# First block's norms taken apart: gains tile by tile, 1/rms later, on other engines

## The chip, the cores and the metric

The kernel runs on one core of a Trainium2 chip. It is a Bass program with one instruction queue per engine: TensorE (PE; its weight loads are PEld), VectorE (DVE), ScalarE (ACT), GpSimd (POOL) and SyncE (SP), which issues the loads. The engines meet only at semaphores. The metric is the device time of one execution in microseconds; three runs of the kernel before gave 1871.84 to 1873.96, median 1873.42.

## The reference, cut to what matters

Two blocks follow each other. The change is in the first: two layers over 272 tokens (16 meta tokens and 256), width 1024, and a closing norm.

```python
def rms_norm(x, g):
    y = xf * lax.rsqrt(jnp.mean(xf * xf, axis=-1, keepdims=True) + NORM_EPS)
    return (y * g.astype(jnp.float32)).astype(x.dtype)

def hybrid_layer(h, pos, norm_g, w_in, ...):
    u = rms_norm(h, norm_g)
    proj = jnp.einsum('bld,dp->blp', u, w_in)
    dq, dk, dv, dz, fq, fk, fv, fz, f_logit = jnp.split(proj, split_points, axis=-1)
    # dq, dk: rope; 4 difference heads. fq, fk: no rope; 8 forgetting heads
    log_f = jax.nn.log_sigmoid(f_logit + b_forget)
    ...
    mixed = jnp.concatenate([o_a * jax.nn.silu(dz), o_b * jax.nn.silu(fz)], axis=-1)
    return h + jnp.einsum('blm,md->bld', mixed, w_out)

for layer in range(DEPTH):                   # DEPTH = 2
    h = hybrid_layer(h, pos, norm_g[layer], ...)
return rms_norm(h, final_g)[:, N_META:]
```

1/rms is one number per token. A projection of u is therefore 1/rms times the projection of x times g.

## The kernel before, in words

**Layout.** Activations are held transposed: features on the 128 partitions, tokens along the free axis, so `hT` is 8 tiles of 128 x 272. 1/rms (`rstd`, 128 x 272) is the same on all partitions.

**Three products for one.** Every projection is made in fp32r from split operands: `whi`, `wlo` of a weight, `uhi`, `ulo` of u, three matmuls per k tile (`three_pass`, lines 420 to 422). ScalarE writes the high half of a weight unit (`split_hi`, line 406) and VectorE the low half (`split_lo`, line 411). Units (up to 1 MB) arrive through a ring of 6 `raw` buffers and are split into a ring of 3: unit n is split once unit n-3 has been used.

**A layer.** Its 33 projection tiles (slots 0 to 32) are pairs of PSUM banks 0 and 1: eight groups of q, k, v, z (gate) and, at slot 12, the forget logits. Groups 0 to 3 are difference heads with rope, 4 to 7 forgetting heads. Tiles 0 and 1 are made together, k tile by k tile, as u appears; later ones each alone, tile i waiting until tile i-2 has been taken out of its bank. ScalarE takes all of them (`take_tile`, signal `proj_taken`): q and k of the difference heads to `qraw`, v to `vt`, fox q and k to `qk`, z twice (`zs` and tanh of its half in `ut`). Rope is TensorE's `rot` product of `qraw` into bank 2, VectorE's product of that with the sine table (`rsn`, line 1387), GpSimd's product of `qraw` with the cosine table (`rc`, line 1796) and VectorE's sum (`qk`, line 1392). At each z slot come the scores of two maps, VectorE's masks and maxima, ScalarE's exponentials, and GpSimd's or VectorE's scaled probabilities, which TensorE turns (line 622) two slots on and multiplies by v. Near the layer's end VectorE takes 1/rms of the difference heads (four reciprocals, line 1482) and mixes.

**Its end.** Eight output tiles (d = 0 to 7) add to `hT` on VectorE (line 1488); units 18 to 23 hold the last six, of 1024 columns each, and the next layer's units 0 and 1 have 2048.

**The norm.** ScalarE squares the eight tiles, TensorE sums them over the features with eight products by a matrix of 1/1024 (`norm_sums`, line 528), ScalarE takes the root (`sd`), VectorE the reciprocal (`rstd`, line 1306). Then for each tile VectorE makes `ut` = x g rstd, ScalarE `uhi`, VectorE `ulo` (`norm_split`, line 1323). Unit 2 is split after that. The closing norm of the block has only the squares, the root and a product (`norm_scale(2)`).

**What sets the order.** All queues are written out by hand, slot by slot; `MAPS_AT`, `TURN_AT`, `MEET_AT`, `MIX_AT` and `RECIP_AT` say at which slot each piece stands. The loop over the layers is a hardware loop.

## Time and profile before

| | us |
|---|---|
| median of three runs | 1873.42 |
| the profiled execution | 1873.47 |
| its span in the trace | 1871.7 |
| TensorE busy | 1737.7 (93%) |
| VectorE busy | 1397.9 (75%) |
| ScalarE busy | 1160.5 (62%) |
| GpSimd busy | 227.6 (12%) |
| first block, to the first square sum of the second | 426.6 |

Times inside the trace count from the start of the span. The shares are means over the whole program; the first block is less than a quarter of it, and the rest (dense and expert layers) is streamed weights.

### The profile page before, as it was taken

How to read it: one execution, taken by the hardware profiler on the slowest of the kernel's cores; microseconds unless marked ns; L12 is line 12 of the kernel's file. 1: busy time of each engine (PE TensorE's matmuls, PEld its weight loads, DVE VectorE, ACT ScalarE, POOL GpSimd, SP SyncE). 2: the span in 40 equal slices, each digit the busy share in tenths (PEclk: the TensorE clock that was granted, in tenths of full speed). 3: DMA queues.
4: the chain of work that ended last, by engine and by line, in shares of the span. 5: the costliest groups of instructions: out<-in, count | busy, mean ns of one | idle time of the engine just before them, and what ended most of it. 6: DMA issues, size and time to landing. Idle time of an engine off the chain costs nothing.

```text
span 1871.7 us, 27995 instructions
## 1 busy us (share of the span) xinstructions
PE 1737.7 (93%) x10004; PEld 1503.7 (80%) x10004; DVE 1397.9 (75%) x1545; ACT 1160.5 (62%) x1306; POOL 227.6 (12%) x230
## 2 busy tenths in 40 slices
PE   5998799988789999887999999999999999999994
PEld 4887698877789998876888888888888888888883
DVE  5655466637765556865889888888888988988886
ACT  5554355545454445654777777777777777777774
POOL 0212022104500000700001000010010100100000
PEclk9999999998899999987999999999999999999997
DMA  6322333143345444343999999999999999999994
GB/s 262 136 80 69 136 136 111 51 160 133 108 163 182 165 156 173 137 153 118 365 369 370 362 366 384 375 368 372 370 372 368 359 380 383 371 356 375 375 372 167
DMA packets 71335, 477.44 MB, mean 255 GB/s; under 512 B 8405, under 2 KB 9077, under 8 KB 19285
## 3 DMA queue, kind: packets, MB, share of 16 engines
q1 hardware_dynamic: 67637, 463.25, 66.2%
q0 software_dynamic: 3328, 12.08, 1.7%
q8 instruction: 48, 0.79, 0.2%
q10 hardware_dynamic: 288, 1.05, 0.1%
q14 instruction: 34, 0.28, 0.0%
HBM read 470.05 MB, written 6.29 MB: 255 GB/s over the span
## 4 chain that ended last, share of the span: by engine, by line
PE 80%; DVE 6%; issue 6%; ACT 4%; POOL 2%; DMA 1%; SPq 0%; DVEq 0%; ACTq 0%; POOLq 0%
PE bank L420 25%; PE bank L422 24%; PE bank L421 24%; ACT whi L406 2%; DVE wlo L411 1%; PE bank L528 1%; PE bank L963 1%; POOL cacc L1857 1%; DVE rstd L1306 1%; DVE msb L1482 1%; PE bank L646 1%; ACT sq L1021 0%; DVE ut L1311 0%; PE bank L935 0%; POOL py L1841 0%
## 5 line engine op out<-in xcount | busy, mean ns | idle before, releaser
L411 DVE TENSOR_TENSOR wlo<-raw,whi 128x2048 fp32r<-128x2048 f32 (+2 forms) x454 | 1009.5, 2228 | 239.4 <-ACT whi L406 237.9
L406 ACT ACTIVATE whi<-raw 128x2048 fp32r<-128x2048 f32 (+2 forms) x454 | 845.2, 1863 | 241.7 <-PE bank L422 239.8
L420 PE MATMUL bank<-whi,hthi 128*128 128x512 f32 x896 | 358.4, 400 | 0.0
L422 PE MATMUL bank<-whi,htlo 128*128 128x512 f32 x896 | 354.1, 395 | 0.0
L421 PE MATMUL bank<-wlo,hthi 128*128 128x512 f32 x896 | 353.9, 395 | 0.0
L420 PE MATMUL bank<-uhi,whi 128*128 128x272 f32 (+2 forms) x1072 | 319.7, 298 | 20.5 <-DVE ulo L1323 20.2
L422 PE MATMUL bank<-uhi,wlo 128*128 128x272 f32 (+2 forms) x1072 | 311.1, 290 | 0.0
L421 PE MATMUL bank<-ulo,whi 128*128 128x272 f32 (+2 forms) x1072 | 310.6, 290 | 0.0
L420 PEld LDWEIGHTS bank<-uhi,whi 128*128 128x128 f32 (+1 forms) x1072 | 207.3, 193 | 24.5 <-issue 22.2
L421 PEld LDWEIGHTS bank<-ulo,whi 128*128 128x128 f32 (+1 forms) x1072 | 207.6, 194 | 0.6
L422 PEld LDWEIGHTS bank<-uhi,wlo 128*128 128x128 f32 (+1 forms) x1072 | 207.0, 193 | 0.0
L422 PEld LDWEIGHTS bank<-whi,htlo 128*128 128x128 f32 x896 | 169.1, 189 | 39.6
L421 PEld LDWEIGHTS bank<-wlo,hthi 128*128 128x128 f32 x896 | 169.4, 189 | 37.5
L420 PEld LDWEIGHTS bank<-whi,hthi 128*128 128x128 f32 x896 | 169.4, 189 | 37.4
L420 PE MATMUL bank<-whi,athi 128*128 128x512 f32 x448 | 179.6, 401 | 0.0
L422 PE MATMUL bank<-whi,atlo 128*128 128x512 f32 x448 | 177.0, 395 | 0.0
L421 PE MATMUL bank<-wlo,athi 128*128 128x512 f32 x448 | 176.7, 394 | 0.0
L1866 POOL TENSOR_TENSOR tick<-one 128x1 f32<-128x1 f32 x27 | 43.4, 1610 | 913.4 <-DVE source_row L1702 494.7
L422 PEld LDWEIGHTS bank<-whi,atlo 128*128 128x128 f32 x448 | 84.3, 188 | 19.8
L421 PEld LDWEIGHTS bank<-wlo,athi 128*128 128x128 f32 x448 | 84.6, 189 | 18.4
L420 PEld LDWEIGHTS bank<-whi,athi 128*128 128x128 f32 x448 | 84.5, 189 | 18.3
L1278 ACT ACTIVATE gsa<-bank 128x512 f32<-128x512 f32 x56 | 33.5, 599 | 48.7 <-PE bank L422 48.7
(294 smaller groups left out, 2098.7 us busy)
## 6 DMA issues: line engine op xcount, KB each, us to landing
raw<-in_wm SPq DMA_DIRECT2D x338, 1024.0 KB, 7.1
raw<-in_w SPq DMA_DIRECT2D x66, 1024.0 KB, 4.8
raw<-in_w SPq DMA_DIRECT2D x18, 768.0 KB, 4.0
raw<-in_w SPq DMA_DIRECT2D x16, 704.0 KB, 3.9
raw<-in_w SPq DMA_DIRECT2D x14, 512.0 KB, 3.5
ys<-y_slots SPq DMA_DIRECT2D x4, 512.0 KB, 5.2
raw<-in_w SPq DMA_DIRECT2D x2, 576.0 KB, 3.6
h_in<-in_hT SPq DMA_DIRECT2D x1, 1088.0 KB, 9.6
```

The lines of the kernel that those rows point to most:

```text
L406: act.activation(whi[:, n % RING, 0:c], raw[:, n % RAW, 0:c], ACT.Copy).then_inc(hi_ready, 1)
L411: dve.tensor_tensor(wlo[:, n % RING, 0:c], raw[:, n % RAW, 0:c], whi[:, n % RING, 0:c].bitcast(F32), ALU.subtract).then_inc(lo_ready, 1)
L420: pe.matmul(out, s_hi, m_hi, start=start, stop=False, skip_group_check=shared)
L421: pe.matmul(out, s_hi, m_lo, start=False, stop=False, skip_group_check=shared)
L422: return pe.matmul(out, s_lo, m_hi, start=False, stop=stop, skip_group_check=shared)
L528: pe.matmul(bank[7][:, 0:n], mean_d[:], sq[:, k % 2, 0:n], start=(k == 0), stop=(k == KD - 1)).then_inc(ms_step, 1)
L646: pe.matmul(b[:, 0:LEN], v01[:, o % 2, 0, c:c + w], pt[:, i, at0:at0 + LEN], start=True, stop=False, skip_group_check=True)
L963: mm = pe.transpose(bank[4][:, i * P:(i + 1) * P], ga[:, c % 2, i * P:(i + 1) * P], ident[:])
L1278: act.activation(gs[:, c % 2, :], bank[c % 2][:], ACT.Silu).then_inc(silu_ready, 1)
L1306: dve.reciprocal(rstd[:], sd[:]).then_inc(rstd_ready, 1)
L1482: dve.reciprocal(msb[:, h, :], msb[:, h, :]).then_inc(subrs_ready, 1)
L1866: pool.tensor_tensor(tick[:, column:column + 1], one[:], one[:], ALU.mult).then_inc(semaphore, 1)
```

## The change

It touches only the first block.

- *x and its gain.* ScalarE writes `uhi` = high half of x g straight from `hT` (`tile_hi`) and squares the same tile; VectorE writes `ulo` = x g - `uhi` (`tile_lo`). No rstd is in it. For layer 2 and the closing norm this is done tile by tile as the output tiles are added to `hT`. The closing norm's `uhi` and `ulo` are written too, though nothing reads them.
- *The sum of squares.* GpSimd adds the eight squares (`acc`, in the buffer of `sd`); TensorE makes one product with the matrix of 1/1024 (`square_sum`), between k tiles 5 and 6 of the first two projection tiles.
- *1/rms.* The projections come out unscaled. VectorE multiplies two sine tables by rstd and GpSimd two cosine tables (`roper`). VectorE takes v, the forget logits and the forgetting heads' q and k with a product by rstd (`take_scaled`, signal `scaled_taken`). ScalarE copies the difference heads' q and k and all z raw (`raw_taken`); GpSimd scales z in place, and ScalarE's tanh follows a slot later (`tanh_half`). The logit's bias is a pass of its own.
- *Order at the start.* Weight unit 0, the gains and x in two halves are loaded first, x directly into `hT`; the reductions for lambda move behind the first splits, their Exp to slot 2. Units 1 and 2 are split before the root.
- *Numbers.* tile i-2's signal now depends on who took it (`tile_taken`). `SPLIT_OUTPUTS` and the waits are recounted.

```diff
+RAW_TAKEN = {i: j for j, i in enumerate(i for i in range(PROJ_T) if TILE_OF[i][0] == "z" or TILE_OF[i][0] in "qk" and TILE_OF[i][1] < DIFF_HEADS)}
+SCALED_TAKEN = {i: j for j, i in enumerate(i for i in range(PROJ_T) if i not in RAW_TAKEN)}
+RAWS, SCALED = len(RAW_TAKEN), len(SCALED_TAKEN)
...
+SUM_AT = KD - 3
+LAM_SLOT = 2
...
+        acc = sd
...
+        def tile_taken(l, i):
+            if i in RAW_TAKEN:
+                return raw_taken, l * RAWS + (RAW_TAKEN[i] + 1)
+            return scaled_taken, l * SCALED + (SCALED_TAKEN[i] + 1)
...
+            load_unit(sp, 0)
+            sp.dma_start(gains[:], io["gains"]).then_inc(in_landed, 16)
+            for i in range(2):
+                ks = slice(i * KD // 2, (i + 1) * KD // 2)
+                sp.dma_start(hT[:, ks, :], io["hT"][:, ks, :]).then_inc(x_landed[i], 16)
+            load_unit(sp, 1)
+            for dst, name in ((rope, "rope"), (rot, "rot"), (ident, "ident"), (bforget, "bforget"), (mask, "mask")):
+                sp.dma_start(dst[:], io[name]).then_inc(par_landed, 16)
             sp.dma_start(lamv, io["lamv"]).then_inc(lam_landed, 16)
             sp.dma_start(subln[:], io["subln"]).then_inc(lam_landed, 16)
-            load_unit(sp, 0)
-            load_unit(sp, 1)
-            sp.dma_start(h_in[:], io["hT"]).then_inc(in_landed, 16)
-            sp.dma_start(gains[:], io["gains"]).then_inc(in_landed, 16)
             load_unit(sp, 2)
-            for dst, name in ((bforget, "bforget"), (rope, "rope"), (rot, "rot"), (ident, "ident"), (mask, "mask")):
-                sp.dma_start(dst[:], io[name]).then_inc(par_landed, 16)
...
+            def square_sum(q):
+                pe.wait_ge(acc_step, q * (KD - 1) + (KD - 1))
+                pe.matmul(bank[7][:, 0:LEN], mean_d[:], acc[:], start=True, stop=True).then_inc(ms_done, 1)
...
+                        if k == SUM_AT:
+                            square_sum(l)
...
-                norm_sums(l, LEN)
...
+            def tile_hi(q, k):
+                gain = gains[:, q:q + 1, k] if isinstance(q, int) else gains[:, bass.ds(q, 1), k]
+                act.activation(uhi[:, k, :], hT[:, k, :], ACT.Copy, scale=gain).then_inc(uhi_ready, 1)
+            def tile_square(q, k):
+                if k >= 2:
+                    act.wait_ge(acc_step, q * (KD - 1) + max(k - 2, 1))
+                act.activation(sq[:, k % 2, :], hT[:, k, :], ACT.Square).then_inc(sq_ready, 1)
+            def root(q):
+                act.wait_ge(ms_done, q + 1)
+                act.activation(sd[:], bank[7][:, 0:LEN], ACT.Sqrt, bias=eps[:]).then_inc(sd_ready, 1)
...
                 if kind == "z":
-                    if g >= 2:
-                        act.wait_ge(zs_ready, l * KD + (g - 1))
-                    act.activation(zs[:, g, :], src, ACT.Copy)
-                    act.activation(ut[:, g % 2, :], src, ACT.Tanh, scale=0.5).then_inc(proj_taken, 1)
+                    act.wait_ge(*tile_done(l, i))
+                    act.activation(zs[:, g, :], bank[i % 2][:, 0:LEN], ACT.Copy).then_inc(raw_taken, 1)
                 elif kind == "logit":
                     act.wait_ge(par_landed, 16 * N_PAR)
-                    act.activation(xb, bank[i % 2][0:FOX_ROWS, 0:LEN], ACT.Identity,
-                                   bias=bforget[:, bass.ds(l, 1)]).then_inc(proj_taken, 1)
-                    act.wait_ge(proj_taken, l * PROJ_T + (i + 1))
+                    act.wait_ge(*tile_taken(l, i))
+                    act.activation(xb, xb, ACT.Identity, bias=bforget[:, bass.ds(l, 1)]).then_inc(logit_step, 1)
+                    act.wait_ge(logit_step, 4 * l + 1)
                     act.activation(ab, xb, ACT.Abs).then_inc(logit_step, 1)
-                    act.wait_ge(logit_step, 3 * l + 1)
-                    act.activation(le, ab, ACT.Exp, scale=-1.0).then_inc(logit_step, 1)
-                    act.wait_ge(logit_step, 3 * l + 2)
-                    act.activation(ll, le, ACT.Ln, bias=one[0:FOX_ROWS, :]).then_inc(logit_step, 1)
-                elif kind == "v":
-                    if g >= 2:
-                        act.wait_ge(vt_done, l * VN + (g - 1))
-                    act.activation(vt[:, g % 2, :], src, ACT.Copy).then_inc(proj_taken, 1)
-                elif g < DIFF_HEADS:
+                    act.wait_ge(logit_step, 4 * l + 2)
+                    act.activation(ab, ab, ACT.Exp, scale=-1.0).then_inc(logit_step, 1)
+                    act.wait_ge(logit_step, 4 * l + 3)
+                    act.activation(ab, ab, ACT.Ln, bias=one[0:FOX_ROWS, :]).then_inc(logit_step, 1)
+                elif i in RAW_TAKEN:
                     r = 2 * g + (kind == "k")
+                    act.wait_ge(*tile_done(l, i))
                     if r >= 2:
                         act.wait_ge(rot_done, l * ROPED + (r - 1))
                         act.wait_ge(rc_ready, l * ROPED + (r - 1))
-                    act.activation(qraw[:, r % 2, :], src, ACT.Copy).then_inc(proj_taken, 1)
-                else:
-                    act.wait_ge(s_done, l * MAPS + 2 * (g - 1))
-                    act.activation(qk[:, 2 * (g % 2) + (kind == "k"), :], src, ACT.Copy,
-                                   scale=-SCALE if kind == "q" else 1.0).then_inc(proj_taken, 1)
+                    act.activation(qraw[:, r % 2, :], bank[i % 2][:, 0:LEN], ACT.Copy).then_inc(raw_taken, 1)
+            def tanh_half(l, i):
+                kind, g = TILE_OF.get(i, ("", 0))
+                if kind == "z":
+                    act.wait_ge(z_scaled, l * KD + (g + 1))
+                    if g >= 2:
+                        act.wait_ge(zs_ready, l * KD + (g - 1))
+                    act.activation(ut[:, g % 2, :], zs[:, g, :], ACT.Tanh, scale=0.5).then_inc(tanh_ready, 1)
...
-            act.wait_ge(lam_step, 2 * LAYERS)
-            act.activation(lame[:], lamp[:], ACT.Exp).then_inc(lam_exp, 1)
+            act.activation(warm[:, 0:1], eps[:], ACT.Sqrt)
             split_hi(act, 0)
+            act.wait_ge(in_landed, 16)
+            for k in range(KD):
+                act.wait_ge(x_landed[k // (KD // 2)], 16)
+                tile_hi(0, k)
+                tile_square(0, k)
             split_hi(act, 1)
             with act.Fori(0, LAYERS) as l:
-                norm_squares(l, LEN, hT, x_ready, 1, l * KD)
-                norm_hi(l, LEN)
                 split_hi(act, 2, l, U1)
+                root(l)
                 for s in range(SLOTS):
+                    tanh_half(l, s - 1)
                     if s < PROJ_T:
                         take_tile(l, s)
+                    if s == LAM_SLOT:
+                        act.wait_ge(lam_step, 2 * LAYERS)
+                        act.activation(lame[:], lamp[:], ACT.Exp).then_inc(lam_exp, 1)
...
-                for u in range(PROJ_U + 1, U1):
-                    split_hi(act, u + 2, l, U1, UNITC if u + 2 >= U1 else None)
-            norm_squares(2, LEN, hT, x_ready, 1, LAYERS * KD)
+                act.activation(warm[:, 1:2], eps[:], ACT.Sqrt)
+                for u in range(PROJ_U, U1):
+                    if u > PROJ_U:
+                        split_hi(act, u + 2, l, U1, UNITC if u + 2 >= U1 else None)
+                    for d in out_tiles(u):
+                        act.wait_ge(x_ready, l * KD + (d + 1))
+                        tile_hi(l + 1, d)
+                        tile_square(l + 1, d)
+            root(2)
...
+            def tile_lo(q, k):
+                gain = gains[:, q:q + 1, k] if isinstance(q, int) else gains[:, bass.ds(q, 1), k]
+                dve.wait_ge(uhi_ready, q * KD + (k + 1))
+                dve.scalar_tensor_tensor(ulo[:, k, :], hT[:, k, :], gain, uhi[:, k, :].bitcast(F32), ALU.mult, ALU.subtract).then_inc(ulo_ready, 1)
...
+            split_lo(dve, 0)
+            for k in range(KD):
+                tile_lo(0, k)
+            split_lo(dve, 1)
...
+            def scaled_tables(l):
+                norm_scale(l)
+                dve.wait_ge(par_landed, 16 * N_PAR)
+                for i in (1, 3):
+                    dve.tensor_tensor(roper[:, i, :], rope[:, i, :], rstd[:], ALU.mult).then_inc(sin_ready, 1)
+                dve.wait_ge(sin_ready, 2 * l + 2)
+            def take_scaled(l, i):
+                if i not in SCALED_TAKEN:
+                    return
+                kind, g = TILE_OF[i]
+                src = bank[i % 2][:, 0:LEN]
+                dve.wait_ge(*tile_done(l, i))
+                if kind == "logit":
+                    op = dve.tensor_tensor(xb, src[0:FOX_ROWS, :], rstd[0:FOX_ROWS, :], ALU.mult)
+                elif kind == "v":
+                    if g >= 2:
+                        dve.wait_ge(vt_done, l * VN + (g - 1))
+                    op = dve.tensor_tensor(vt[:, g % 2, :], src, rstd[:], ALU.mult)
+                else:
+                    dve.wait_ge(s_done, l * MAPS + 2 * (g - 1))
+                    op = dve.scalar_tensor_tensor(qk[:, 2 * (g % 2) + (kind == "k"), :], src, -SCALE if kind == "q" else 1.0, rstd[:],
+                                                  ALU.mult, ALU.mult)
+                op.then_inc(scaled_taken, 1)
...
-                norm_split(l, l, hT, LEN)
                 split_lo(dve, 2, l, U1)
+                scaled_tables(l)
                 for s in range(SLOTS):
+                    if s < PROJ_T:
+                        take_scaled(l, s)
                     turned(l, s - 1)
...
+                        if d:
+                            tile_lo(l + 1, d - 1)
+                tile_lo(l + 1, KD - 1)
...
+            def square_adds(q):
+                for k in range(1, KD):
+                    pool.wait_ge(sq_ready, q * KD + (k + 1))
+                    if k > 1:
+                        pool.wait_ge(acc_step, q * (KD - 1) + (k - 1))
+                    pool.tensor_tensor(acc[:], acc[:] if k > 1 else sq[:, 0, :], sq[:, k % 2, :], ALU.add).then_inc(acc_step, 1)
+            pool.wait_ge(const_ready, 1)
+            square_adds(0)
             pool.wait_ge(par_landed, 16 * N_PAR)
             with pool.Fori(0, LAYERS) as l:
+                pool.wait_ge(rstd_ready, l + 1)
+                for i in (0, 2):
+                    pool.tensor_tensor(roper[:, i, :], rope[:, i, :], rstd[:], ALU.mult).then_inc(cos_ready, 1)
+                pool.wait_ge(cos_ready, 2 * l + 2)
                 for s in range(SLOTS):
                     kind, g = TILE_OF.get(s, ("", 0))
...
+                    if kind == "z":
+                        pool.wait_ge(*tile_taken(l, s))
+                        pool.tensor_tensor(zs[:, g, :], zs[:, g, :], rstd[:], ALU.mult).then_inc(z_scaled, 1)
...
+                square_adds(l + 1)
```

**ScalarE near the end of a layer.** `whi` is a unit's high half, `uhi` and `sq` belong to an output tile. Before, the last 1024-column unit and the next layer's units 0 and 1:

```order
L405 REGISTER_ALU [waits raw_landed5]
L406 ACTIVATE whi<-raw 128x1024 [waits unit_done]
L403 REGISTER_ALU
L405 REGISTER_ALU [waits raw_landed0]
L406 ACTIVATE whi<-raw 128x2048 [waits unit_done]
L405 REGISTER_ALU [waits raw_landed1]
L406 ACTIVATE whi<-raw 128x2048 [waits unit_done]
```

Now the same place:

```order
L414 REGISTER_ALU [waits raw_landed5]
L415 ACTIVATE whi<-raw 128x1024 [waits unit_done]
L1063 ISA [waits x_ready]
L1063 ACTIVATE uhi<-hT,gains 128x272
L1068 REGISTER_ALU
L1069 ACTIVATE sq<-hT 128x272 [waits acc_step]
L412 REGISTER_ALU
L414 REGISTER_ALU [waits raw_landed0]
L415 ACTIVATE whi<-raw 128x2048 [waits unit_done]
L1063 ISA [waits x_ready]
L1063 ACTIVATE uhi<-hT,gains 128x272
```

Between two splits now stand a wait for the residual sum (`x_ready`), the copy and the square.

**VectorE at the same place.** `wlo` is a unit's low half, `hT` the residual sum. Before:

```order
L410 REGISTER_ALU
L411 TENSOR_TENSOR wlo<-raw,whi 128x1024 [waits hi_ready]
L1488 TENSOR_TENSOR hT<-hT,bank0 128x272 [waits unit_done]
L410 REGISTER_ALU
L411 TENSOR_TENSOR wlo<-raw,whi 128x2048 [waits hi_ready]
L1488 TENSOR_TENSOR hT<-hT,bank3 128x272 [waits unit_done]
```

Now:

```order
L419 REGISTER_ALU
L420 TENSOR_TENSOR wlo<-raw,whi 128x1024 [waits hi_ready]
L1573 TENSOR_TENSOR hT<-hT,bank0 128x272 [waits unit_done]
L1366 REGISTER_ALU
L1367 ISA [waits uhi_ready]
L1367 SCALAR_TENSOR_TENSOR ulo<-hT,gains,uhi 128x272
L419 REGISTER_ALU
L420 TENSOR_TENSOR wlo<-raw,whi 128x2048 [waits hi_ready]
L1573 TENSOR_TENSOR hT<-hT,bank3 128x272 [waits unit_done]
L1366 REGISTER_ALU
L1367 ISA [waits uhi_ready]
L1367 SCALAR_TENSOR_TENSOR ulo<-hT,gains,uhi 128x272
```

The residual sum stood behind the low half already; the low half of u of the tile before has come in behind it.

**VectorE at slots 26 and 27 of a layer** (group 6; `vt` is its v, bank 1 is tile 27). Before:

```order
L1449 TENSOR_TENSOR mx32<-osb,zs 128x272 [waits sub_ready]
L410 REGISTER_ALU
L411 TENSOR_TENSOR wlo<-raw,whi 128x2048 [waits hi_ready]
L1453 TENSOR_TENSOR mixlo<-mx32,mixhi 128x272 [waits mixhi_ready]
L1482 RECIPROCAL msb<-msb 128x272 [waits subsd_ready]
L1447 ISA [waits subrs_ready,zs_ready,mixlo_ready]
L1447 SCALAR_TENSOR_TENSOR osb<-osb,subg,msb 128x272
L1449 TENSOR_TENSOR mx32<-osb,zs 128x272 [waits sub_ready]
```

Now:

```order
L1526 TENSOR_TENSOR mx32<-osb,zs 128x272 [waits sub_ready]
L419 REGISTER_ALU
L420 TENSOR_TENSOR wlo<-raw,whi 128x2048 [waits hi_ready]
L1530 TENSOR_TENSOR mixlo<-mx32,mixhi 128x272 [waits mixhi_ready]
L1567 RECIPROCAL msb<-msb 128x272 [waits subsd_ready]
L1443 REGISTER_ALU
L1449 TENSOR_TENSOR vt<-bank1,rstd 128x272 [waits vt_done,half_done]
L1524 ISA [waits subrs_ready,zs_ready,mixlo_ready]
L1524 SCALAR_TENSOR_TENSOR osb<-osb,subg,msb 128x272
L1526 TENSOR_TENSOR mx32<-osb,zs 128x272 [waits sub_ready]
```

VectorE now takes v between a reciprocal and the product `osb`; before, ScalarE took it.

## Rows read from the trace of the kernel before

**Rows 1.** Windows; columns: stretch, length, busy PE, PEld, DVE, ACT, POOL (instructions), clock, DMA share, GB/s.

```profile
0.00:43.33 43.33, 22.99 (x132) 18.93 (x132) 25.27 (x60) 19.96 (x30) 3.53 (x6) 0.96 0.70 267
43.33:199.57 156.24, 146.43 (x1105) 132.46 (x1106) 86.28 (x234) 79.73 (x210) 29.53 (x42) 0.98 0.26 93
199.57:244.70 45.13, 35.88 (x234) 32.15 (x232) 28.31 (x39) 22.37 (x32) 3.32 (x2) 0.92 0.45 164
...
400.95:426.60 25.65, 19.33 (x118) 16.62 (x116) 15.17 (x18) 13.57 (x20) 0.00 (x0) 0.91 0.62 226
```

**Rows 2.** Waits of TensorE, 0 to 216: total us, times, longest.

```profile
PE bank L528 <- ACT sq L1021: 15.5, 1, 15.5
PE bank L622 <- POOL pr L1785: 4.6, 2, 3.5
...
PE bank L622 <- DVE pr L1432: 2.3, 1, 2.3
```

**Rows 3.** Timeline, start; columns: start, us, engine, line, operation, out<-in, [idle before <-releaser].

```profile
0.75 0.69 SPq L464 DMA_DIRECT2D ex<-in_lamv  x1
...
2.12 0.91 SPq L399 DMA_DIRECT2D raw<-in_w  x2
...
4.06 0.22 DVE L1338 CUSTOM_DVE_ANT_0 rsn<-ex 128x64 f32<-128x64 f32 x1 [1.37 <-DMA subln<-in_subln]
...
8.07 1.91 ACT L406 ACTIVATE whi<-raw 128x2048 fp32r<-128x2048 f32 x1 [1.40 <-DMA raw<-in_w]
```

**Rows 4.** Chain of waits, start: the scores before tile 4.

```profile
42.27 1.05 PE bank L588 x12
```

**Rows 5.** Timeline, VectorE, end of layer 1.

```profile
199.57 0.78 DVE L1488 TENSOR_TENSOR hT<-hT,bank 128x272 f32<-128x272 f32 x2 [1.11 <-PE bank L422]
200.66 1.23 DVE L411 TENSOR_TENSOR wlo<-raw,whi 128x1024 fp32r<-128x1024 f32 x1 [0.31 <-ACT whi L406]
...
214.86 2.29 DVE L411 TENSOR_TENSOR wlo<-raw,whi 128x2048 fp32r<-128x2048 f32 x1 [0.39 <-ACT whi L406]
217.07 0.43 DVE L1488 TENSOR_TENSOR hT<-hT,bank 128x272 f32<-128x272 f32 x1
```

**Rows 6.** Timeline, ScalarE, end of layer 1, and the closing norm's root.

```profile
199.57 2.95 ACT L406 ACTIVATE whi<-raw 128x1024 fp32r<-128x1024 f32 x3 [1.59 <-PE bank L422]
...
209.88 1.92 ACT L406 ACTIVATE whi<-raw 128x2048 fp32r<-128x2048 f32 x1 [2.12 <-PE bank L422]
212.90 1.92 ACT L406 ACTIVATE whi<-raw 128x2048 fp32r<-128x2048 f32 x1 [1.11 <-PE bank L422]
...
217.90 0.73 ACT L1021 ACTIVATE sq<-hT 128x272 f32<-128x272 f32 x2
...
423.23 0.49 ACT L1023 ACTIVATE sd<-bank,eps 128x272 f32<-128x272 f32 x1 [0.82 <-PE bank L528]
```

**Rows 7.** Timeline, GpSimd, rope products of layer 1.

```profile
34.74 3.33 POOL L1796 TENSOR_TENSOR rc<-qraw,rope 128x272 f32<-128x272 f32 x2 [34.28 <-ACT qraw L1065]
...
50.82 1.50 POOL L1796 TENSOR_TENSOR rc<-qraw,rope 128x272 f32<-128x272 f32 x2
```

**Rows 8.** Timeline, VectorE, beside the first of those.

```profile
34.41 2.29 DVE L411 TENSOR_TENSOR wlo<-raw,whi 128x2048 fp32r<-128x2048 f32 x1 [1.36 <-ACT whi L406]
...
37.44 0.93 DVE L1392 TENSOR_TENSOR qk<-rc,rsn 128x272 f32<-128x272 f32 x1 [0.39 <-POOL rc L1796]
```

**Rows 9.** Timeline, VectorE, a reciprocal at slot 26.

```profile
155.61 1.84 DVE L1482 RECIPROCAL msb<-msb 128x272 f32<-128x272 f32 x1
```

**Rows 10.** Timeline, ScalarE, slots 27 and 28.

```profile
152.92 0.38 ACT L1059 ACTIVATE vt<-bank 128x272 f32<-128x272 f32 x1
...
162.65 0.29 ACT L1081 ACTIVATE ex<-sm,nmax 16x16 f32<-16x16 f32 x1
```

**Rows 11.** Timeline, TensorE, slot 28.

```profile
154.47 0.27 PE L574 MATMUL bank<-ident,vt 128*16 128x128 f32 x1
...
157.63 0.21 PE L607 MATMUL bank<-kcum,ncum 40*16 40x16 f32 x4
```

More of the change, by code:

```diff
@@ L251, in build_program @@
         lame = sb("lame", [P, LAYERS, 2], scope=first)
-        lamd = sb("lamd", [P, LAYERS], scope=first)
+        lam0 = sb("lam0", [P, LAYERS], scope=first)
         lam = sb("lam", [P, LAYERS], scope=first)
-        xb, ab, lf, le, ll = (logits[:, i, :] for i in range(5))
+        xb, ab, lf = (logits[:, i, :] for i in range(3))
         first.close()
@@ L340, in build_program @@
         in_landed, par_landed = sem("in_landed"), sem("par_landed")
+        x_landed = [sem(f"x_landed{i}") for i in range(2)]
+        acc_step, ms_done, cos_ready, sin_ready = sem("acc_step"), sem("ms_done"), sem("cos_ready"), sem("sin_ready")
+        raw_taken, scaled_taken, tanh_ready = sem("raw_taken"), sem("scaled_taken"), sem("tanh_ready")
+        z_scaled = sem("z_scaled")
         lam_landed, par2_landed = sem("lam_landed"), sem("par2_landed")
@@ L435, in unit_starting, with tile_done @@
             return u if s == 0 else None
+        def tile_taken(l, i):
+            if i in RAW_TAKEN:
+                return raw_taken, l * RAWS + (RAW_TAKEN[i] + 1)
+            return scaled_taken, l * SCALED + (SCALED_TAKEN[i] + 1)
+        def tile_done(l, i):
+            u, half = proj_place(i)
+            if half == U1_TILES[u] - 1:
+                return unit_done, l * U1 + (u + 1)
+            return half_done, l * PAIRS + (u - (u > LOGIT_U) + 1)
         def out_bank(d):
@@ L1031, in take_tile @@
+            def tile_square(q, k):
[5 more added lines that the diff above has]
+                act.activation(sd[:], bank[7][:, 0:LEN], ACT.Sqrt, bias=eps[:]).then_inc(sd_ready, 1)
             def take_tile(l, i):
-                src = bank[i % 2][:, 0:LEN]
                 kind, g = TILE_OF[i]
-                u, half = proj_place(i)
@@ L1340, in _ @@
                     dve.wait_ge(lam_step, 2 * l + i + 1)
[L1341 to L1343 removed]
             for l in range(LAYERS):
[L1345 removed]
+                dve.memset(lam0[:, l:l + 1], LAMBDA_INIT[l]).then_inc(lam_ready, 1)
                 dve.tensor_scalar(subg[:, l, :], subln[:, l, :], 0.5 * (1.0 - LAMBDA_INIT[l]), None, ALU.mult).then_inc(lam_ready, 1)
[L1347 to L1352 removed]
+            dve.wait_ge(lam_ready, 2 * LAYERS)
             def key_cum(l, f):
@@ L1386, in turned @@
                         dve.wait_ge(roped, l * ROPED + r)
-                    dve.tensor_tensor(rsn[:], bank[2][:, 0:LEN], rope[:, 2 * (r % 2) + 1, :], ALU.mult).then_inc(turn_taken, 1)
+                    dve.tensor_tensor(rsn[:], bank[2][:, 0:LEN], roper[:, 2 * (r % 2) + 1, :], ALU.mult).then_inc(turn_taken, 1)
                     dve.wait_ge(turn_taken, l * TURNS + (TURN_USES["rot", r] + 1))
@@ L1456, in _ @@
             with dve.Fori(0, LAYERS) as l:
-                norm_split(l, l, hT, LEN)
                 split_lo(dve, 2, l, U1)
+                scaled_tables(l)
                 for s in range(SLOTS):
+                    if s < PROJ_T:
+                        take_scaled(l, s)
                     turned(l, s - 1)
+                    if s == LAM_SLOT + 1:
+                        dve.wait_ge(lam_exp, l + 1)
+                        for j in range(LAYERS):
+                            op = dve.scalar_tensor_tensor(lam[:, j:j + 1], lame[:, j, 0:1], lam0[:, j:j + 1], lame[:, j, 1:2], ALU.add, ALU.subtract)
+                        op.then_inc(lam_ready, 1)
+                        dve.wait_ge(lam_ready, 2 * LAYERS + 1 + l)
                     if s in SUMS_AT:
```

58 lines of the change are left out of this document (20 added, 38 removed).

## The prediction

> **What bounds the kernel now.** I read the profile in this order: the page's busy shares, the windows cut where the first block's stages begin and end, TensorE's waits, the chain of waits at those cuts, and then VectorE's, ScalarE's and GpSimd's timelines around them. The page says TensorE 93% busy over the whole span, so a change in the first block only counts where TensorE is *not* kept busy. The windows show where that is [rows 1]. Layer 1's inside (slot 4 on, up to the first finished output tiles, 43.33 to 199.57) keeps TensorE busy 146.43 of 156.24 us. The three norm stages do not: the start has 22.99 of 43.33, the passage into layer 2 has 35.88 of 45.13, the passage into the second block 19.33 of 25.65. Layer 2's inside repeats layer 1's within 0.01 us, and what comes after 426.60 (1445.10 us) isn't touched. TensorE's waits name the causes [rows 2]: 15.5 us for the first square, and inside a layer only waits for turned probabilities (2.3 and 3.5 us the largest). So the sum has five terms: start, two insides, two passages.
>
> **Start (43.33 to about 35.5: -7.8).** Today VectorE's first reduction, and a 256 KB load, stand ahead of weight unit 0, whose split starts at 8.07 [rows 3]. Now unit 0 is issued at 0.75 instead of 2.12 and x comes behind it in halves, ahead of unit 1 [rows 3]. With 1.4 us saved in issue and that load no longer ahead, I put unit 0 at 6.4 and x's halves at about 8.2 and 9.8 (0.56 MB each, at 267 GB/s of the stretch 2 us, at the peak seen less). Then:
> - ScalarE: unit 0's high half 6.4 to 8.3; per tile a scaled copy and a square. A Copy with a scale operand should cost like the root with its bias operand, 0.49; two squares back to back take 0.73 [rows 6], so about 0.75 a tile.
> - VectorE: unit 0's low half to 10.6 (2.29), then eight low halves of u at 0.44. GpSimd: seven adds. A 272-column GpSimd product takes 0.75 when undisturbed (two in 1.50) [rows 7]. But one begun at 34.74 while VectorE ran a two-operand SBUF split (34.41 to 36.70) took about 2.6 of the 3.33 us that two took [rows 7, 8], and a VectorE sum that met the next product took 0.93 instead of 0.44 [rows 8]. They exclude each other. So from 10.6 on, an add and a low half share one lane: 1.27 us a pair, seven pairs, and the last add ends near 19.0 (in parallel it would be 17.8).
> - TensorE now asks for the sum between tiles 5 and 6, gets it at 19.0, has the mean at 19.9 and both first tiles at 21.4. That comes far earlier than today, but it is not the gain.
> - What is late next is rstd. ScalarE splits units 1 and 2 before the root (18.8, 20.7; root ends 21.2). VectorE has low half 1 (21.1), the lambda reductions, which moved behind it (four like the one at 4.06, with constants 1.4 us: 22.5), low half 2 (24.8), the reciprocal (1.84, as the one of the same size in [rows 9]; 26.7), then two sine tables against GpSimd's two cosine tables, again one lane: 2 x 0.44 + 2 x 0.75 = 2.4 (29.2). GpSimd's first product then ends 30.0, the roped q 30.9, low half 3 33.1, v is taken 33.5, roped k 34.4, scores 1.05: tile 4 starts at 35.5. Today it starts at 43.33, behind the scores of 42.27 [rows 4]. -7.8; between -5 (x or unit 0 2.8 us later than I place them) and -10 (no collisions).
>
> Here the Trainium skill bears: "SBUF — State Buffer", section "Who interferes with whom", says that a VectorE instruction with two SBUF inputs and a GpSimd instruction that reads SBUF take turns, the second being fully blocked. The trace agrees in both directions; by a reading without it the start would be -10.
>
> **End of a layer, the term that decides.** Today ScalarE splits the next units as TensorE frees them, beside VectorE's residual sums. The order of the changed kernel shows one ring instead: ScalarE's split of unit u+2, VectorE's low half, *then* its residual sum of tile d (it stands behind the low half in its queue), then ScalarE's copy and square of d, and only then the split of u+3. From rows: 1024 columns: ScalarE's start to VectorE's start 1.09, low half to residual 1.14 (its 1.23 less the 0.08 by which such neighbours overlap), residual 0.46, copy and square 0.73: 3.42 us a turn. 2048 columns: 1.96 (212.90 to 214.86) + 2.21 (to 217.07) + 0.46 + 0.73 = 5.36 [rows 5, 6]. It starts at 200.0, after the first residual, with two tiles (1.5), so the splits begin at 201.5, 204.9, 208.3, 211.8, 215.2 and 220.5. The last residual ends 220.5 + 1.96 + 2.21 + 0.43 = 225.1, against 217.5 now: 7.6 us later. TensorE's output tiles themselves hardly suffer (tile 4 starts 203.8, not 202.02; the last ends 217.7, not 215.9).
>
> **Passage into layer 2 (-4.0).** Last square 226.0, last add 226.8, mean 227.6, first tiles 229.1. ScalarE splits unit 2 at 225.9 to 227.8, root 228.4; low half 2 230.1, reciprocal 231.9, tables 234.4, rope product 235.2, roped q 236.1, low half 3 238.3, v 238.7, roped k 239.6, scores 240.7. Today tile 4 starts at 244.70, the end of the third stretch. Bounds: 0 (if TensorE's new gaps hold it at the lower clock level; the granted clock of this stretch is 0.92 today, of the insides 0.98 [rows 1]) and -7 (no collisions, ring 2 us shorter).
>
> **Passage into block 2 (+5.8).** Nothing of u is wanted here: only the square sum is. The same ring puts the root at 227.6 + 201.4 = 429.0. Today the squares run at once after the last residual and the root starts at 423.23 [rows 6]. A loss, because eight copies, eight low halves and the ring stand before it. Bounds +3 and +8.
>
> **Insides (+1.9 each).** Taking q, k, v with VectorE costs 0.44 each for ScalarE's 0.38; what counts is the place in the queue. *Logit*: it is taken by VectorE, then a bias pass (0.49) is added before Abs, Exp and Ln, and the unit split and the probabilities behind it end TensorE's 2.3 us wait. About 1.0 later, less the 0.3 that the moved tanh gives: +0.7 (0 to 1.7). *Tile 27 (v of group 6)*: ScalarE took it at 152.92, TensorE turned it at 154.47 and had the scores at 157.8 [rows 10, 11]. VectorE takes it after a low half, mixlo and the 1.84 us reciprocal of 155.61, itself 0.8 late through tiles 25 and 26: 158.6. Transposes, values and scores (3.4 us) then end at 162.0; exponentials that began at 162.65 begin near 163.9, behind masks and a split [rows 9 to 11]. Of 4.1 us of TensorE wait, about 2.9 comes out of its later 3.5 us wait for probabilities, so +1.2 (0 to 4.1). The other takes, as I place them, come 0.7 us or more before TensorE wants the bank again; I price them at nothing, since TensorE's next tile of 3.0 us (209.88 to 212.90 [rows 6]) covers them, and at 0.44 each where it doesn't. Gate tiles: GpSimd's 0.75 product lies beside ScalarE's exponentials of the same slot, so nothing. Table loads: one for Exp at slot 2 in place of the one for tanh at slot 3.
>
> **Sum.** -7.8 + 1.9 - 4.0 + 1.9 + 5.8 = -2.2. The profiled execution took 1873.47 (span 1871.7 and 1.8 around it), the median of the runs is 1873.42: 1871.3 us.
>
> **Rivals.**
> - *The insides hide everything.* For it: TensorE waits 10 us in each inside, so 1.9 could drown; ScalarE loses work. Against: both sit on the chains of exactly those waits. -6.0: 1867.5. Chance 0.22.
> - *The ring doesn't bind* (residual sums get ahead of the low halves). For it: no engine alone has more than about 3.2 us of work in a 3.0 us tile. Against: the order. Both ends 7.6 better: -17.4, 1856. Chance 0.07.
> - *Slower: VectorE's queue paces all four forgetting groups.* Place: the v takes of tiles 19, 23 and 31 as well as 27, in both layers. For it: three more instructions a group, and GpSimd's gate products block two-operand ones. Against: VectorE is 86 us busy of 156. At the 1.2 us of tile 27, six more are +7.2: 1878.5. It decides the sign from 1.0 us each. Chance 0.18.
> - *The scaling isn't what is waited for after the start* (x or unit 0 comes late): +2.8, 1874.1; within my own range.
>
> **Numbers.** My case has 0.53 and runs from 1868 to 1876. Under 0.2% (3.7 us) a measurement of this kernel can't tell a change. Faster than 1869.7: 0.19 of the first rival, 0.07, and 0.06 of mine: 0.32. Slower than 1877.2: 0.13 of the third and 0.05 of mine: 0.18. Same: 0.50. Range 1862 to 1880: from between the first two rivals to just past the third.
>
> **What would show it.** Right: the chain at layer end alternating whi, wlo, hT, uhi, sq with about 3.4 and 5.4 us a turn; the last hT sum 7 to 8 us after where it stood; the final root 5 to 6 us later within its stretch; TensorE waiting for VectorE's v of tile 27; project(4) at 35 to 36. Wrong: hT sums directly after TensorE's tiles; the rope tables not on the chain at the start; an inside longer by more than 4 us, or shorter.

## The result and the profile after

The changed kernel takes 1880.83 us (median of 6 runs, 1874.72 to 1882.48) against 1873.42: slower, ratio 1.0035 with a 95% interval of 1.0024 to 1.0046. One of the six executions of the kernel before beside it took 3450.61 us and doesn't count in this. The profiled execution has a span of 1879.0 us against 1871.7, so +7.3. I had forecast 1871.3 (-2.2), with a range up to 1880: wrong in sign and just outside.

The same windows as [rows 1], cut at the same events: project(4), first finished output tile, project(4) of layer 2, first output tile, first mean of the second block. Columns as there.

```profile
0.00:33.34 33.34, 17.46 (x117) 16.10 (x117) 25.18 (x48) 19.80 (x29) 10.46 (x16) 1.00 0.87 341
33.34:193.61 160.27, 149.17 (x1109) 134.20 (x1106) 92.15 (x251) 74.85 (x195) 34.60 (x49) 0.96 0.26 92
193.61:240.19 46.58, 34.08 (x219) 32.34 (x217) 27.26 (x36) 22.38 (x31) 9.64 (x12) 0.85 0.45 158
240.19:400.70 160.51, 149.41 (x1109) 134.47 (x1106) 92.07 (x251) 74.83 (x195) 34.59 (x49) 0.96 0.26 90
400.70:433.57 32.87, 16.86 (x104) 15.64 (x102) 18.66 (x26) 15.07 (x26) 5.39 (x7) 0.76 0.51 176
433.57:1879.00 1445.43, 1365.55 (x7316) 1170.29 (x7316) 1156.48 (x961) 944.79 (x807) 159.53 (x138) 0.96 0.78 293
```

Against [rows 1], stretch by stretch:

| Stretch | before | after | measured | forecast |
|---|---|---|---|---|
| start | 43.33 | 33.34 | -10.0 | -7.8 |
| inside layer 1 | 156.24 | 160.27 | +4.0 | +1.9 |
| passage into layer 2 | 45.13 | 46.58 | +1.5 | -4.0 |
| inside layer 2 | 156.25 | 160.51 | +4.3 | +1.9 |
| passage into block 2 | 25.65 | 32.87 | +7.2 | +5.8 |
| rest | 1445.10 | 1445.43 | +0.3 | 0 |
| sum | | | +7.3 | -2.2 |

Every term but the first came out worse. TensorE's waits from 193.61 on name two of the causes, VectorE's v of tile 27 and GpSimd's last add (total us, times, longest), where [rows 2] had neither.

```profile
PE bank L551 <- POOL sd L1881: 8.9, 1, 8.9
PE bank L429 <- DVE wlo L420: 7.4, 2, 3.7
PE bank L600 <- ACT qraw L1098: 4.3, 2, 3.8
PE bank L429 <- DVE ulo L1367: 3.9, 1, 3.9
PE bank L605 <- DVE vt L1449: 3.8, 1, 3.8
```

**End of layer 1.** One turn of the ring in the chain of waits (start, us, what; its longest pieces), where [rows 5, 6] had residual sums directly after TensorE's tiles:

```profile
201.42 0.44 DVE hT L1573
202.08 0.34 issue
202.42 0.41 ACT sq L1069
202.83 0.96 ACT whi L415
204.08 0.88 issue
204.96 0.44 DVE hT L1573
```

From residual sum to residual sum it is 3.54 us a turn with a small unit (3.42 forecast) and 5.46 with a large one (5.36). The reader sees residual sum, square, split, and a stretch called issue before the next sum. That last one is VectorE's low half: it starts 1.0 us after the split does, and its 1.2 us end where the sum begins.

**ScalarE behind it**, the timeline up to the root (answers to [rows 6]):

```profile
219.97 0.53 ACT L1063 ACTIVATE uhi<-hT,gains 128x272 fp32r<-128x272 f32 x1 [2.81 <-DVE hT L1573]
220.40 0.41 ACT L1069 ACTIVATE sq<-hT 128x272 f32<-128x272 f32 x1
225.20 1.91 ACT L415 ACTIVATE whi<-raw 128x2048 fp32r<-128x2048 f32 x1 [4.39 <-issue]
227.02 0.47 ACT L1074 ACTIVATE sd<-bank,eps 128x272 f32<-128x272 f32 x1
```

I had the split of unit 2 begin at once. ScalarE stands still 4.39 us, waiting for nothing that the profile shows. Between the square and that split stands the jump back to the start of the layer loop.

**Inside a layer**, TensorE (timeline, then windows of 4 us: length, busy PE, granted clock, DMA share, GB/s). The v of tile 27 is late as forecast; what I had not priced is the clock behind it:

```profile
150.72 0.28 PE L605 MATMUL bank<-ident,vt 128*16 128x128 f32 x1 [3.79 <-DVE vt L1449]
```
```profile
145.34:149.34 4.00, 1.59 (x13) 1.00 0.00 0
149.34:153.34 4.00, 2.62 (x11) 0.75 0.39 135
153.34:157.34 4.00, 4.00 (x29) 0.50 0.00 0
157.34:161.34 4.00, 4.00 (x31) 0.89 0.01 2
```

### The profile page after: what moved, and what is told of

Its sections match the earlier page's. It is cut to its first block, busy times and chain, and to the rows that moved or that the text cites. A ratio compares the mean times of both kernels' runs of the same rounds, so it can differ in the third digit from the quotient of the medians.

```text
span 1879.0 us, 27995 instructions
## 1 busy us (share of the span) xinstructions
PE 1732.5 (92%) x9962; PEld 1503.0 (80%) x9962; DVE 1411.8 (75%) x1570; ACT 1151.7 (61%) x1282; POOL 254.2 (14%) x271
## 4 chain that ended last, share of the span: by engine, by line
PE 79%; issue 8%; DVE 5%; ACT 4%; POOL 3%; DMA 1%; DVEq 0%; ACTq 0%; POOLq 0%; SPq 0%
PE bank L429 25%; PE bank L431 24%; PE bank L430 24%; ACT whi L415 2%; PE bank L993 1%; POOL cacc L1963 1%; PE bank L557 1%; PE bank L677 1%; DVE wlo L420 1%; DVE rstd L1356 0%; PE bank L619 0%; PE bank L965 0%; POOL py L1947 0%; ACT sq L1069 0%; DVE msb L1567 0%
```

## Experiments

All are timed against the kernel before in the same rounds (its medians there 1872.6 to 1873.5). For comparison, the changed kernel's ratio is 1.0035. The cuts are the same as above.

**1. ScalarE's jump.**

```diff
-            with act.Fori(0, LAYERS) as l:
+            for l in range(LAYERS):
```

> The changed kernel with ScalarE's layer loop written out twice instead of run as a hardware loop; nothing else differs. In the changed kernel ScalarE sits idle 4.39 us (220.8 to 225.20, put down to issue) between the last square of layer 1 and the split of unit 2. Theory A (the jump back to the loop's start, after which ScalarE's instructions have to come in again, costs this time, and it now lies on the path to the reciprocal): the idle stretch shrinks under 0.5 us, the passage into layer 2 goes from 46.6 to about 42.2 us, all other stretches stay within 0.3: 4.4 us faster than the changed kernel, about 1876.4 where that runs 1880.8. Rival B (ScalarE really waits there for weight unit 2 or for TensorE to free its ring slot, which the profile doesn't name): the idle stretch stays at 4.4, no change. Rival C (the time goes, but VectorE's and GpSimd's own loops jump at the same place and become late instead): 1 to 2 us.

Measured: 1876.82 us, ratio 1.0022 (1.0013 to 1.003). ScalarE's idle stretch is gone: the split of unit 2 follows the square at 219.39 and the root runs at 221.52. But VectorE now has one of its own, at the same place in the program:

```profile
219.29 0.50 DVE L1367 SCALAR_TENSOR_TENSOR ulo<-hT,gains,uhi 128x272 fp32r<-128x272 f32 x1 [0.28 <-ACT uhi L1063]
224.58 2.29 DVE L420 TENSOR_TENSOR wlo<-raw,whi 128x2048 fp32r<-128x2048 f32 x1 [4.78 <-issue]
```

So the passage fell only from 46.58 to 45.05: rival C, with theory A's cause; 2.4 us in all by the ratios. Another 0.7 and 0.9 us came back in the insides (160.27 and 160.51 to 159.62 each) and 0.6 in each ring (25.80 to 25.18 from first to last residual sum). Waits there now compare with constants; I did not separate that from other effects.

**2. The ring.** At the layer's end, the split ahead of the previous unit's copy and square:

```diff
                     if u > PROJ_U:
                         split_hi(act, u + 2, l, U1, UNITC if u + 2 >= U1 else None)
-                    for d in out_tiles(u):
+                    for d in (out_tiles(u - 1) if u > PROJ_U else ()):
                         ...
+                for d in out_tiles(U1 - 1):
+                    ...
```

> The changed kernel with one edit on ScalarE: at the end of a layer the scaled copy and the square of a finished output tile are issued one unit later, behind the split of the next weight unit, so that no split waits for a residual sum. VectorE's order (low half, then residual sum) stays. Theory A (the ring split, low half, residual sum, copy and square, next split sets the pace at both layer ends, 8.3 us each: 25.8 us from first to last residual sum against 17.5 before): first to last residual sum falls to 17.5 to 19 us in both layers; the passage into layer 2 goes from 46.6 to about 39, the one into block 2 from 32.9 to about 25.5, in all 14 to 15 us faster than the changed kernel, about 1866.5. Rival B (VectorE's low half ahead of the residual sum, or TensorE itself, paces it nearly as much): under 4 us in all. Rival C (the splits go early, but copies and squares pile up behind the last tile): 4 to 10 us. The idle 4.4 us of ScalarE at the loop's jump should stay.

Measured: 1863.53 us, ratio 0.995 (0.9937 to 0.9963), 15.9 us under the changed kernel by the ratios. First to last residual sum 16.96 us in both layers. The passages are 37.21 and 24.05, 9.4 and 8.8 shorter:

```profile
194.89:232.10 37.21, 30.39 (x220) 28.59 (x218) 27.32 (x36) 22.82 (x31) 14.15 (x12) 0.95 0.53 193
392.49:416.54 24.05, 14.36 (x104) 13.14 (x102) 19.17 (x26) 15.21 (x26) 9.92 (x7) 0.90 0.66 241
```

The two large splits now wait for TensorE freeing a ring place, 0.95 and 0.37 us, and not for a residual sum. The small ones follow a copy that waited 0.26 us for its sum at most, where it was 1.74:

```profile
203.17 0.42 ACT L1069 ACTIVATE sq<-hT 128x272 f32<-128x272 f32 x1
204.54 1.92 ACT L415 ACTIVATE whi<-raw 128x2048 fp32r<-128x2048 f32 x1 [0.95 <-PE bank L431]
206.37 0.50 ACT L1063 ACTIVATE uhi<-hT,gains 128x272 fp32r<-128x272 f32 x1
206.78 0.41 ACT L1069 ACTIVATE sq<-hT 128x272 f32<-128x272 f32 x1
207.57 1.92 ACT L415 ACTIVATE whi<-raw 128x2048 fp32r<-128x2048 f32 x1 [0.37 <-PE bank L431]
```

Theory A holds, a little beyond its figures. From first to last residual sum each layer's end got 8.8 us shorter (25.80 to 16.96), which is nearly all that the passages gained. The granted clock of the two passages rose too, from 0.85 and 0.76 to 0.95 and 0.90; what that gave by itself no run separates.

**3. Tile 27.** On VectorE, in slots 23 to 26:

```diff
+                    if s in RECIP_AT:
+                        ...
                     if (u := unit_starting(s + 1)) is not None:
                         split_lo(dve, u + 2, l, U1)
                     ...
-                    if s in RECIP_AT:
-                        ...
```

> The changed kernel with one edit on VectorE: in slots 23 to 26 the 1.84 us reciprocal stands ahead of the low half of the next weight unit instead of behind it, where VectorE sits idle 2.3 us for ScalarE's split. Theory A (TensorE's wait of 3.79 us in each layer for the v of tile 27 is VectorE's queue, and this wait together with the low clock after it is what makes an inside 160.3 us instead of 156.2): the wait falls to about 1.9, the granted clock after it recovers sooner, each inside gets 1.5 to 3 us shorter, 3 to 6 us in all, about 1876.5. Rival B (the chain only moves: TensorE's later wait for turned probabilities, 3.5 us at the same place in the kernel before and gone in the changed one, comes back by as much): insides unchanged within 0.5 us, total within 1 us. Rival C (tile 27 isn't late through the reciprocal): the wait stays at 3.8.

Measured: 1871.93 us, ratio 0.9993 (0.9984 to 1.0002), some 7.9 us under the changed kernel by the ratios, more than theory A's 3 to 6. The insides are 156.92 and 155.85 instead of 160.27 and 160.51, and the wait for the v of tile 27 has left TensorE's list. The first row is from the changed kernel, the others from this run:

```profile
PE bank L653 <- POOL pr L1873: 1.4, 2, 1.1
...
PE bank L653 <- POOL pr L1873: 3.3, 2, 3.1
PE bank L653 <- DVE pr L1509: 2.6, 1, 2.6
PE bank L429 <- DVE mixlo L1530: 2.0, 2, 1.5
```

In the windows, layer 2's inside has TensorE busy 146.44 us where it was 149.41, for the same 1109 records, at a clock of 0.98 instead of 0.96:

```profile
34.53:191.45 156.92, 147.51 (x1109) 133.35 (x1106) 92.21 (x252) 76.02 (x196) 35.14 (x49) 0.97 0.26 90
238.18:394.03 155.85, 146.44 (x1109) 132.01 (x1106) 91.92 (x250) 75.07 (x195) 35.12 (x49) 0.98 0.27 94
```

So of 4.7 us there, 3.0 are busy time, the same matmuls at a higher clock, and 1.7 are idle time. Layer 1 gained 3.4, half of it (149.17 to 147.51) busy time. Rival B (the chain only moves) is half right: the wait of 3.5 us after tile 27 didn't come back, but an earlier one for GpSimd's probabilities grew from 1.13 to 3.08 us, so of the 3.79 us about 1.9 are gone.

**4. The loads.** The old order of the first loads in the changed kernel:

```diff
+            sp.dma_start(lamv, io["lamv"]).then_inc(lam_landed, 16)
+            sp.dma_start(subln[:], io["subln"]).then_inc(lam_landed, 16)
             load_unit(sp, 0)
+            load_unit(sp, 1)
             sp.dma_start(gains[:], io["gains"]).then_inc(in_landed, 16)
             ...
-            load_unit(sp, 1)
```

> The changed kernel with the order of the first loads of the kernel before (lambda vectors, units 0 and 1, then gains and x, in halves); VectorE's lambda reductions stay behind unit 1's low half, the computation stays the new one. Theory A (about half of the 10.0 us that the start gained comes from x and unit 0 landing earlier, the rest from no longer waiting for the mean before splitting u): x lands near 12.8 instead of 7.5, the start goes from 33.3 to 37 to 38.5, 4 to 5 us slower than the changed kernel, about 1885. Rival B (the gain is all in the computation, since the squares' sum isn't waited for early on): under 1 us. Rival C (it is all in the loads): 9 us or more.

Measured: 1885.15 us, ratio 1.0056 (1.0042 to 1.0071), 3.9 us above the changed kernel by the ratios. The start is 38.99 us in the profiled execution, the slowest of the six (1888.27 us). Measured in this way, the loads are worth 5.65 of the 10.0 and the computation 4.3: theory A, a little above its range of 37 to 38.5. The opposite order, new loads with the old computation, was not run. x is taken at 12.69, as forecast for the old order:

```profile
12.69 0.52 ACT L1063 ACTIVATE uhi<-hT,gains 128x272 fp32r<-128x272 f32 x1 [2.17 <-DMA hT<-in_hT]
```

**5. All jumps.** The layer loop of all five engines written out, in the changed kernel and in the kernel before (the edit of experiment 1, five times):

> The changed kernel with the layer loop of all five engines written out twice. With ScalarE's alone written out, ScalarE's 4.39 us of issue at the passage into layer 2 went, but VectorE then sat 4.78 us in issue at the same place and TensorE 3.6. Theory A (each engine pays some 4 to 5 us at its own jump back, and the last of them is what the passage waits for): with none left, no engine shows an issue gap over 0.5 us there, the passage goes from 46.6 (45.05 with ScalarE's alone) to about 41, and the total, with the 0.7 us each that constant waits gave back in the other stretches, lies 8 us under the changed kernel, about 1871.5 where before runs 1872.6. Rival B (the gap on VectorE and TensorE isn't the jump but code that comes in late anyway): the gaps stay, passage 45, total like ScalarE's alone (1876.8). Rival C (the longer straight code costs instruction fetches elsewhere): a gain at the passage that is lost in the insides.

> The kernel before with the layer loop of all five engines written out twice. In the changed kernel this edit gave 5.8 us at the passage into layer 2 and 7 us in all. Theory A (before, the jumps lay mostly beside work that the passage waited for anyway: only ScalarE's 1.67 us of issue at 214.8 to 216.50 stood ahead of the squares): passage 1.7 us shorter, 43.4 instead of 45.1, with small gains from constant waits 2 to 4 us in all. Rival B (the jump cost before just as much, so the change did not expose anything): passage 5 us or more shorter, total 6 us or more faster than before.

Measured, changed kernel: 1873.97 us, ratio 1.0002 (0.9993 to 1.0011), 6.2 us under it by the ratios. No engine has an issue gap at the passage, which is 40.79 us (41 forecast); VectorE's low half of unit 2 now waits 1.61 us, for ScalarE's split:

```profile
192.16:232.95 40.79, 30.54 (x220) 28.66 (x218) 26.88 (x36) 22.53 (x31) 9.62 (x12) 0.96 0.51 176
```
```profile
220.47 2.29 DVE L420 TENSOR_TENSOR wlo<-raw,whi 128x2048 fp32r<-128x2048 f32 x1 [1.61 <-ACT whi L415]
```

Measured, kernel before: 1870.36 us, ratio 0.9985 (0.9976 to 0.9994), passage 43.25 instead of 45.07 (45.13 in [rows 1], whose cut lies 0.06 later): 1.8 us. Its profiled execution was its slowest, 1874.64 us; only the passage is read from it. Theory A holds in both, though the changed kernel gained 6.2 us in all where I had 8. The loops cost the changed kernel 5.8 us at this passage, 0.6 of them in the ring (25.80 to 25.17), and the kernel before 1.8; the change exposed 4.0 us.

**6. Is experiment 3 a repair?** The same edit in the kernel before.

> The kernel before, with only the reciprocals of slots 23 to 26 ahead of the low half on VectorE. It tells whether that edit repairs what the change did to tile 27 or is a gain of its own. Theory A (it repairs the change: before, ScalarE took this v at once and the reciprocal delayed nothing that TensorE waited for; its 3.5 us wait for turned probabilities at 167.58 comes from the probabilities' own chain): within 1 us of before. Rival B (the reciprocal also stood on the chain of that 3.5 us wait): 2 to 4 us faster per run, since each layer's wait falls by 1 to 1.8.

Measured: 1869.73 us, ratio 0.9982 (0.9973 to 0.9991), insides 154.80 and 154.79 instead of 156.3. TensorE's waits for GpSimd's probabilities sum to 3.1 us where they were 4.6. Rival B: some 3.4 us of the 7.9 would have been there without the change, and about 4.5 undo what the change did.

**7. Together, and one edit more.** Edits 2 and 3; then with all loops written out; then also the norm's reciprocal and tables ahead of unit 2's low half:

```diff
-                split_lo(dve, 2, l, U1)
                 scaled_tables(l)
+                split_lo(dve, 2, l, U1)
```

> The changed kernel with both edits together that helped alone: ScalarE's copy and square one unit later at a layer's end (alone 1863.5) and VectorE's reciprocals ahead of the low half in slots 23 to 26 (alone 1871.9, against some 1879 to 1881 for the changed kernel). Theory A (they sit in different stretches and add up): 1856 to 1857. Rival B (what one gives back is what the other gave, through the clock or the queue at slot 32): over 1860.

> The changed kernel with all three edits: copies and squares one unit later, reciprocals ahead of the low half, all layer loops written out. If the third edit adds what it should, 5.5 us at the passage and some 2 us in the rest, 1849 to 1851; if the jump is hidden again once the layer's end is no longer a ring (ScalarE is free earlier), only 1 to 3 us less than the two edits, 1854.

> The changed kernel with copies and squares one unit later, reciprocals ahead of the low half and all loops written out (1850.6 where before ran 1873.2), and now VectorE's reciprocal of the norm and its two sine tables ahead of unit 2's low half instead of behind it, at the start and at the passage. Theory A (what is late at the start and at the passage is 1/rms on VectorE, behind a 2.29 us low half that TensorE needs only for tile 4): each gets 1 to 2.2 us shorter, 2 to 4 us in all, about 1847.5. Rival B (the low half is then what tile 4 or the first scores wait for, since it sits ahead of the rotated q): within 1 us.

Measured: 1855.99 us, ratio 0.9907 (0.9892 to 0.9922), so the edits add up. With the loops: 1850.58 us, 0.9873 (0.9858 to 0.9889), as forecast. This version beats both kernels, the one before by 1.3%. With the tables first: 1849.4 us, 0.9875 (0.986 to 0.989), no difference: rival B in size. At the start the tables do begin 2.3 us sooner (22.36 for 24.69), but GpSimd's two rope products now run beside that low half and take 3.40 us instead of 1.50, which I had not named:

```profile
23.76 2.74 DVE L420 TENSOR_TENSOR wlo<-raw,whi 128x2048 fp32r<-128x2048 f32 x1
```
```profile
24.43 3.40 POOL L1902 TENSOR_TENSOR rc<-qraw,roper 128x272 f32<-128x272 f32 x2
```

The first roped q follows only 0.4 us sooner (27.22 for 27.61), and the start is 33.59 us for 33.20. The products take 3.40 us at the passage too, which is still 0.8 us shorter (33.35 for 34.14); but the insides are 155.35 and 155.25 for 154.54 and 153.50. Why these grew isn't shown.

The windows of the version with three edits, in the order of the table above:

```profile
0.00:33.20 33.20, 18.47 (x117) 17.45 (x117) 25.27 (x48) 18.78 (x29) 10.40 (x16) 0.95 0.88 346
33.20:187.74 154.54, 145.78 (x1109) 131.94 (x1106) 92.56 (x251) 75.78 (x196) 34.67 (x49) 0.98 0.28 94
187.74:221.88 34.14, 29.98 (x219) 28.54 (x218) 27.38 (x36) 22.66 (x31) 14.46 (x12) 0.95 0.60 209
221.88:375.38 153.50, 144.74 (x1109) 131.19 (x1106) 92.15 (x251) 74.86 (x195) 34.65 (x49) 0.99 0.27 95
375.38:400.24 24.86, 15.34 (x105) 14.46 (x103) 19.18 (x26) 15.09 (x26) 10.20 (x7) 0.86 0.67 233
```

## Why the prediction was wrong

**Start: mechanism right, size 2.2 us short.** The order of events was as told. Unit 0 was there at 5.8 (I had 6.4; and seven pairs of 1.27 us from 10.6 on end at 19.5, not at the 19.0 that I wrote). The low halves and adds excluded each other less than I charged:

```profile
9.31 1.32 POOL L1881 TENSOR_TENSOR sd<-sq 128x272 f32<-128x272 f32 x1 [8.85 <-ACT sq L1069]
11.18 5.46 POOL L1881 TENSOR_TENSOR sd<-sd,sq 128x272 f32<-128x272 f32 x6 [0.55 <-ACT sq L1069]
```

Six adds in 5.46 us are 0.91 a pair, not my 1.27, and the last ended at 16.64 instead of 19.0. The tables took 2.1 us for 2.4.

**End of a layer: right.** The turns measured 3.54 and 5.46 for 3.42 and 5.36. The residual sums end 8.3 us later within the stage (25.80 for 17.50) where I had 7.6, and taking the ring away gave the time back (experiment 2).

**Passage into layer 2: this step failed.** The prediction let ScalarE split unit 2 at 225.9, right after the last square. Counted from the first output tile, that is 26.3 us; it came at 31.6. From there to project(4) I had 14.8 us and it took 15.0. Of the miss of 5.5 us, 4.4 lie between two neighbouring instructions of one engine, and experiments 1 and 5 show what it is: the jump back of each engine's layer loop, which the prediction put at nothing without a word. Before, only 1.67 us of ScalarE's stood ahead of the squares (up to 216.50), and the other engines show no issue there, only waits for the squares and the root (TensorE 2.48 us, VectorE 6.52). The change moved the squares ahead of the jump and left only the split, the root and the reciprocal behind it, so nothing covers it any more. The forecast gives the passage 41.1 us; with all loops written out it is 40.79, so the loops cover the whole miss. In the comparison with the kernel before, 4.0 us are newly exposed and 1.8 were in its 45.1 already, where my forecast counted them as gained. The split of the 5.8 us into the idle time itself, the 0.6 us of ring and the clock (0.85, and 0.96 without the loops) isn't shown. My bound of 0 at worst was too narrow, since it held no term for the loop.

**Insides: causes right; the step that failed is the price of a TensorE wait.** The two places were the ones named: the wait for probabilities after the logit (2.58 for 2.30, with 0.55 for the rotated q before it), and tile 27 (3.79; I had 4.1). Their idle time came to +1.3 of the forecast +1.9: TensorE idles 11.1 us in layer 1 (160.27 less 149.17) against 9.8. But its busy time grew by 2.7 us with the same work, since the granted clock was 0.96 instead of 0.98. That term I had at nothing. Both places have it. After the 3.79 us wait the windows above have 0.75, 0.50 and 0.89, together 3.4 us of full clock lost (4 us times what each is short of 1.00) at the lower of the two levels, 1.2 GHz; before, after a 3.50 us wait, it was 0.75 and 0.82, or 1.7 us. After the wait behind the logit it was 3.5 us for 1.7. Summed over an inside, 6.9 us for 3.4.

The length of the wait doesn't say how much is lost. In layer 2 the same 3.79 us wait, at 356.36, cost 5.1 us:

```profile
354.98:358.98 4.00, 2.62 (x9) 0.65 0.41 135
358.98:362.98 4.00, 4.00 (x28) 0.50 0.00 0
362.98:366.98 4.00, 4.00 (x21) 0.57 0.00 0
```

The 2.58 us wait behind the logit cost 1.7 there and 3.5 in layer 1. I had costed TensorE's waits in time alone.

**Passage into block 2: right in cause, 1.4 us short.** The root came 29.5 us after the first output tile (28.05 by my reckoning, 22.3 before): 0.7 from the ring, most of the rest from the one matmul of the mean. It ran at the lower clock after an 8.88 us pause, 1.27 us long, where the same one at 221.92 took 0.62.

**Rivals.** The third named the right sign and nearly the size (1878.5), for a wrong reason: beyond tile 27 no TensorE wait of layer 1's inside names VectorE's take of a v. The first (the insides hide everything) fell with the insides' +4.0. The second, of no ring, is what experiment 2 built: 15.9 us better than the changed kernel, where the rival put 15.2 between the two. It lies only 9.4 us under the kernel before, not 17.4, because the jumps and the insides were mis-sized there too. The fourth (x or unit 0 late) didn't happen.

## What to carry to other kernels

When work is moved across the end of a loop, look at what stands directly behind the jump on each engine: it is late by the jump, and only what was already slack there hides it. Where a queue takes finished tiles and also prepares the next ones, prepare first: here one unit's distance was worth 16 us. A wait of TensorE inside a busy stretch cost more than its length here, by 1.7 to 5.1 us of full clock, so the forecast from waits alone came out too low.

## What the runs showed of the hardware

At a hardware loop's jump back an engine stood idle for some 4 us: 4.39 us on ScalarE, 4.78 on VectorE once ScalarE's was gone, and 3.57 on TensorE in that same run, all put down to issue, and none of them with the loops written out. In the kernel before ScalarE's showed as 1.67 us. Transfers of the instruction queues stand in this window of the trace (q14: 4 packets between 222 and 228 us, none there with the loops written out), which fits instructions that are fetched anew; that they cause the gap is argued, not shown.

GpSimd's rope products took 3.40 us instead of 1.50 beside a 2.74 us VectorE low half. This agrees with the exclusion that the prediction drew on, and at the start it ate what the last edit gained. Between short instructions of both engines it was milder than a full exclusion: 0.91 us a pair at the start, where one of each alone takes 0.50 and 0.77.
